# Two transformer blocks on one core: the mixing stage put into another order, attention ahead of the convolution

## What is computed

```python
x = x + 0.5 * swiglu(rms_norm(x, ffn1_norm[l]), ...)
h = rms_norm(x, mix_norm[l])
a, g, q, k, v = jnp.split(h @ w_in[l], splits, axis=-1)
# convolution branch: causal, per channel, 31 taps
u = a * jax.nn.sigmoid(g)
conv_out = jax.nn.silu(rms_norm(conv(u) + conv_b, conv_norm))
# attention branch: 4 heads, each with two score maps (d = 64), v of 128 columns
q, k = rms_norm(q, q_norm[l]), rms_norm(k, k_norm[l])
p = softmax(q @ k.T * scale + bias)          # causal, per head and map
o = (p[:, :, 0] - lam * p[:, :, 1]) @ v
diff_out = rms_norm(o, subln_g) * (1.0 - lam_init)
x = x + concat([conv_out, diff_out]) @ w_out[l]
x = x + 0.5 * swiglu(rms_norm(x, ffn2_norm[l]), ...)
```

## Time and profile before

| | us |
|---|---|
| median of 3 runs (1810.07 to 1811.17) | 1810.5 |
| the profiled execution, whole | 1811.22 |
| its span in the trace | 1809.4 |
| PE busy | 1758.0 (97%) |
| DVE busy | 1208.4 (67%) |
| ACT busy | 911.7 (50%) |
| POOL busy | 287.7 (16%) |
| granted TensorE clock, mean over the span | 0.992 |

### The profile page before, as it was taken

One profiled execution on the slowest core, in us unless ns is written; L12 is line 12 of the kernel. 1 busy time (PEld: TensorE's weight loads), 2 busy tenths in 40 slices (PEclk: granted clock), 3 DMA queues, 4 the chain that ended last, 5 costly groups with the idle time before them and its releaser, 6 DMA issues.

```text
span 1809.4 us, 25402 instructions
## 1 busy us (share of the span) xinstructions
PE 1758.0 (97%) x9839; PEld 1502.4 (83%) x9839; DVE 1208.4 (67%) x1594; ACT 911.7 (50%) x1221; POOL 287.7 (16%) x155
## 2 busy tenths in 40 slices
PE   8999999999999999999999998999999999989999
PEld 7757888899897788878888977888888889778887
DVE  5756766778676775576665794666666667946665
ACT  4544444545455444445445656544554456565443
POOL 2000300376241040000000741000000006410000
PEclk9999999999999999999999999999999999999999
DMA  9223655554502576535554432655465554316552
GB/s 302 102 70 124 220 191 186 152 181 156 198 1 83 156 238 194 188 129 195 194 193 163 164 116 70 209 185 188 161 209 185 186 185 164 117 47 209 192 194 102
DMA packets 203965, 293.95 MB, mean 162 GB/s; under 512 B 6426, under 2 KB 169728, under 8 KB 203888
## 3 DMA queue, kind: packets, MB, share of 16 engines
q1 hardware_dynamic: 200768, 285.62, 47.6%
q0 software_dynamic: 2688, 6.47, 1.4%
q10 hardware_dynamic: 432, 0.79, 0.1%
HBM read 291.81 MB, written 1.05 MB: 162 GB/s over the span
## 4 chain that ended last, share of the span: by engine, by line
PE 87%; DVE 8%; ACT 3%; issue 1%; DMA 0%; POOL 0%; SPq 0%; ACTq 0%; DVEq 0%
PE acc L1864 27%; PE pg L1864 15%; PE pg L1927 12%; PE pg L1931 12%; PE pg L1930 6%; PE pg L1928 6%; PE acc L2338 1%; DVE acc L1743 1%; PE pg L2134 1%; ACT w_hi L793 1%; DVE w_lo L1252 1%; PE pg L2322 1%; PE pg L2324 1%; DVE stats L1307 1%; PE pg L1975 1%
## 5 line engine op out<-in xcount | busy, mean ns | idle before, releaser
L1252 DVE TENSOR_TENSOR w_lo<-w_raw,w_hi 128x2048 fp32r<-128x2048 f32 x231 | 539.1, 2334 | 182.2 <-ACT w_hi L793 170.6
L793 ACT CAST w_hi<-w_raw 128x2048 fp32r<-128x2048 f32 x270 | 515.6, 1910 | 68.5 <-PE pg L1864 25.2
L1864 PE MATMUL acc<-w_hi,op 128*128 128x512 f32 x1536 | 496.6, 394 | 8.2 <-DVE op L1829 6.4
L1927 PE MATMUL pg<-op,w_hi 128*128 128x512 f32 x960 | 383.2, 399 | 7.7 <-DVE op L1278 3.8
L1931 PE MATMUL pg<-op,w_hi 128*128 128x512 f32 x960 | 380.8, 397 | 0.0
L1864 PEld LDWEIGHTS acc<-w_hi,op 128*128 128x128 f32 x1536 | 290.4, 189 | 70.0 <-issue 12.6
L1864 PE MATMUL acc<-w_lo,op 128*128 128x512 f32 x768 | 300.7, 392 | 0.0
L695 POOL TENSOR_TENSOR w_lo<-w_raw,w_hi 128x2048 fp32r<-128x2048 f32 x39 | 179.8, 4613 | 743.5 <-DVE w_lo L1252 615.4
L1930 PE MATMUL pg<-op,w_lo 128*128 128x256 f32 x960 | 267.9, 279 | 0.0
L1928 PE MATMUL pg<-op,w_lo 128*128 128x256 f32 x960 | 267.0, 278 | 0.0
L1864 PE MATMUL pg<-op,w_hi 128*128 128x256 f32 x1232 | 229.2, 286 | 2.8 <-DVE op L1278 1.2
(11 more groups left out here) (314 smaller groups left out, 1845.2 us busy)
## 6 DMA issues: line engine op xcount, KB each, us to landing
w_raw<-in_mlp_w SPq DMA_DIRECT2D x64, 1024.0 KB, 5.5
w_raw<-in_ffn_w_gate SPq DMA_DIRECT2D x44, 1024.0 KB, 5.1
w_raw<-in_ffn_w_up SPq DMA_DIRECT2D x44, 1024.0 KB, 5.1
w_raw<-in_ffn_w_down SPq DMA_DIRECT2D x44, 1024.0 KB, 4.8
w_raw<-in_ssm_w_in SPq DMA_DIRECT2D x24, 1024.0 KB, 5.3
w_raw<-in_w_in SPq DMA_DIRECT2D x20, 1024.0 KB, 5.0
w_raw<-in_attn_w_in SPq DMA_DIRECT2D x9, 1024.0 KB, 9.2
w_raw<-in_ssm_w_out SPq DMA_DIRECT2D x8, 1024.0 KB, 4.8
```

Of the source, the lines that this page charges most:

```text
L793: act.copy(w_hi[:, u % RING, :], w_raw[:, u % RING, :]).then_inc(hi_ready, 1)
L1252: dve.tensor_tensor(w_lo[:, s, :], w_raw[:, s, :], w_hi[:, s, :].bitcast(F32), ALU.subtract) \
L1864: ins = pe.matmul(psum, l, r, start=first and i == 0, stop=last and i == 2)
L1927: pe.matmul(bank, hi, joined, start=k == 0, stop=False)
```

## The change

The order of the units and of all four engines' programs in the mixing stage is new:

```diff
-MIX_COLS = [2 * U, 0, 3 * U, U] + [2 * CCH + i * U for i in (0, 2, 1, 3, 4, 5)]
-TAPS = [24, 22, 8, 8, 8, 8, 5, 5, 5]
-PE_TAPS = 6
-DIAGS = [0, 10, 20, CK]
+MIX_COLS = [2 * U, 0] + [2 * CCH + i * U for i in (0, 2, 1, 3)] + [3 * U, U] + [2 * CCH + i * U for i in (4, 5)]
+DIAGS = [0, 8, 16, 24, CK]
...
-                for n in range(OUT_UNITS):
-                    load(U_MIX_OUT[l] + n, rows(v_mix_out[l], n))
+                for n, g in enumerate((2, 3, 0, 1)):
+                    load(U_MIX_OUT[l] + n, rows(v_mix_out[l], g))
```

PE's program, the part that sets the order:

```diff
-                for s in range(2 * DH + 6):
-                    i = 8 * l + s
-                    if s < 2 * DH:
...
+                    if n == 6:
+                        score2(1)
+                    if n == 7:
+                        score2(3)
+                    feature_chunk(u, bank[:, T:2 * T], 1).then_inc(unit_done, 1)
+                    if n == 5:
+                        score2(0)
+                    if n == 6:
+                        score2(2)
+                        key_spread(2 * l + 1)
+                score2(4)
...
+                wide_tile(u, 0, acc[:, 0, :], 0)
+                score2(5)
+                pe.wait_ge(qk_ready, 2 * l + 2)
+                wide_tile(u, 0, acc[:, 1, :], 1).then_inc(unit_done, 1)
+                mix_turn(0)
+                score2(6)
+                take(u + 1)
+                wide_tile(u + 1, 1, acc[:, 0, :], 0).then_inc(first_tile, 1)
+                mix_turn(1)
+                score2(7)
+                wide_tile(u + 1, 1, acc[:, 1, :], 1).then_inc(unit_done, 1)
+                conv_taps(0, 4)
+                o2(l, 0)
+                mix_turn(2)
+                o2(l, 1)
```

DVE's and ACT's programs beside it, and block 1's two splits on ACT:

```diff
+                score_step(3)
+                mix_head(0)
                 gated_columns(1)
...
+                score_step(4)
+                mix_head(1)
+                convolve(3)
+                score_step(5)
+                convolve(4)
+                score_step(6)
+                convolve(2)
+                mix_head(2)
+                score_step(7)
...
+                gate_columns(1)
+                exp_step(0)
+                exp_step(1)
+                exp_step(2)
+                split(U_MIX[l] + 9)
+                exp_step(3)
+                split(U_MIX_OUT[l])
+                exp_step(4)
+                exp_step(5)
+                turned_mix(0)
+                split(U_MIX_OUT[l] + 1)
+                exp_step(6)
...
-                if s == AQ + 2:
-                    split(U_ATT_OUT + 2)
-                if s == AQ + 7:
-                    split(U_ATT_OUT + 3)
...
+                if s == 14:
+                    split(U_ATT_OUT + 2)
+                if s == 16:
+                    split(U_ATT_OUT + 3)
```

More of the change, by code:

```diff
@@ new lines, in _ @@
+                turned_mix(1)
+                exp_step(7)
+                link(act.activation(part[:, 0:1], lnb[:, 0:1], ACT.Sqrt))
+                act.wait_ge(unit_done, U_MIX[l] + 10)
+                act.copy(V2[:, 1, :], acc[:, 1, :]).then_inc(v_ready, 1)
+                turned_mix(2)
+                turned_mix(3)
+                o2_square(l, 0)
+                o2_square(l, 1)
+                o2_high(l, 0)
+                o2_high(l, 1)
+                split(U_MIX_OUT[l] + 2)
+                act.wait_ge(pe_conv, l + 1)
@@ new lines, in mix_turn, with conv_taps @@
+                def mix_turn(h):
+                    k = DH * l + h
+                    pe.wait_ge(mix_ready, k + 1)
+                    if h == 0:
+                        pe.wait_ge(gate_ready, 2 * l + 2)
+                    if k >= 1:
+                        pe.wait_ge(mixT_ready, k)
+                    for o in (0, P, 2 * P):
+                        ins = pe.transpose(pg[:, 2, o:o + P], pmix[:, k % 2, o:o + P], ident[:, :])
+                    ins.then_inc(mixT_done, 1)
+                def conv_taps(k0, k1):
+                    for k in range(k0, k1):
+                        if k == 0:
+                            pe.wait_ge(u_ready, 4 * l + 4)
+                        if k in DIAGS:
+                            pe.wait_ge(diag_ready, 4 * l + DIAGS.index(k) + 1)
+                        ins = pe.matmul(pg[:, 3, 0:T], diag_tap(k), uu[:, 3, k:k + T], start=k == 0, stop=k == CK - 1)
+                    if k1 == CK:
+                        ins.then_inc(pe_conv, 1)
@@ L2456, in _ @@
[L2456 to L2470 removed]
+                    elif n in (6, 7):
+                        pe.wait_ge(qk_sq, 4 * l + n - 5)
@@ new lines, in _ @@
+                    bank = pg[:, n % 4, :]
+                    if n < 3:
+                        project(u, bank, fresh=f"mix_{l}" if n == 0 else None)
+                        continue
+                    take(u)
+                    feature_chunk(u, bank[:, 0:T], 0)
+                    if n < 7:
+                        qk_sums(4 * l + n - 3)
+                    if n == 5:
+                        key_spread(2 * l)
+                    if n == 6:
+                        score2(1)
+                    if n == 7:
+                        score2(3)
@@ new lines, in _ @@
+                mix_turn(3)
+                o2(l, 2)
+                conv_taps(8, 12)
+                o2(l, 3)
+                conv_taps(12, 24)
+                o2_turn(0)
+                conv_taps(24, CK)
+                o2_turn(1)
+                u = U_MIX_OUT[l]
+                take(u)
+                pe.wait_ge(o2_ready, 2 * l + 1)
+                for i in (0, 1, 4, 5):
+                    output_part(u, 12, i, True, False)
+                pe.wait_ge(csq, 2 * l + 2)
+                for t in range(TT):
+                    for c in range(4):
+                        ins = pe.matmul(pg[:, 1, t:t + 1], osq[:, c, t * P:(t + 1) * P], ones_m,
+                                        start=c == 0, stop=c == 3)
@@ new lines, in _ @@
+                ins.then_inc(csum, 1)
+                take(u + 1)
+                pe.wait_ge(o2_ready, 2 * l + 2)
+                for i in (0, 1, 4, 5):
+                    output_part(u + 1, 14, i, False, False)
+                pe.wait_ge(crstd, l + 1)
+                for t in range(TT):
+                    ins = pe.matmul(pg[:, 1, T + t * P:T + (t + 1) * P], cdev[:, t:t + 1].broadcast_to([P, P]),
+                                    ident[:, :], start=True, stop=True)
+                ins.then_inc(cspread, 1)
```

564 lines of the change are left out of this document (286 added, 278 removed).

## The result

The changed kernel takes **1834.4 us** (median of 4 runs, 1834.14 to 1834.71) against 1810.8 for the kernel before, measured beside it: a ratio of 1.0131 (95% interval 1.0113 to 1.0148). The forecast was 1831, within 1814 to 1842.

The account below looks back on a forecast made before the run. PE, busy 97% of the span, bounds the kernel. 2 x (7.5 stage + 1.2 second feed-forward start + 2 slow clock) - 1 for block 1 = +20.4 on 1811.2 gives 1831.6; median 0.7 lower, 1831, range 1814 to 1842.

Parts of the forecast that it names:

- What decides: DVE beside POOL: DVE instructions reading data from SBUF alone wait for POOL's running subtraction, up to 4.6 us.
- Where it blocks: Scores among projections: multiplies L1832 and L1839 wait 4.4 and 4.6 us, L1832 of head 2 waits 3.4.
- its own sign of being wrong: If multiply L1832 is never above 0.5 us in the changed profile, the reason and the sign are wrong.
- PE's waits: Mixing stage to the out-projection's end: 3.6 + 2.7 + 1.1 + 3.3 + 7.3 + 3.1 = 21.1 us for 13.5.
- The stage's length: Mixing stage: out-projection ends at 133.5 for 126.0 in the layout, +7.5; about 135 to 139 us behind the warm-up.
- Slow clock: +2: Mixing stage, per layer: five waits of 2.7 to 7.3 us, about 5 us lost for 3; bounds 0 and 5.
- Block 1: PE's waits of 1.91 and 2.26 us behind casts that move later: -1 us, once; bounds -4.2 and +3.8.
- The turn: Start of the mixing stage: +0.2 us; PE waits 3.6 in place of 1.1 and works 1.8 less.
- PE's work: Mixing stage, per layer: 0 us, short matmuls of the sums taken at 0.11 each; lower end -4.
- The last taps: Convolution: chunk 2's last seven taps behind the attention's low halves, sums at 111.9 for 108.7, +3.1 us.
- The first (no block bites): Rival: DVE's multiplies start just before POOL or small ones pass; 1797 to 1808, say 1803; chance 0.15.
- The third (more bite): Rival: a lower clock moves steps into other subtractions; 5 us more a layer, 1842; chance 0.10.

Follow-up runs that it names:

- without POOL's length: Changed kernel with POOL subtracting only 8 of 2048 columns of each weight unit of the mixing stages, order and semaphores kept: 1807.4 us.
- the combined kernel: Changed kernel with three weight subtractions on DVE, the last seven taps early and ACT's root table load behind its copy of V: 1805.8 us.
- the last kernel: The combined kernel with the old turn, score steps earlier on DVE and chunk 2's taps dealt out around the attention's norm: 1795.7 us.

## Why the prediction was right, point by point

- **What decides.** Right, and shown: DVE's multiplies with source and destination in SBUF wait for POOL's subtraction, PE waits behind them (27 us between the changed kernel with and without POOL's length, 0.9 and within the noise in the kernel before). The prediction named the Trainium skill for it ("SBUF — State Buffer", section "Who interferes with whom"). By that rule the case agrees, with 0.16 us for a PSUM source and 3.78 for an SBUF source under one subtraction.
- **Where it blocks.** The size was right, the instruction was not: I laid 4.4 and 4.6 us on the mix of head 0 and 3.4 on that of head 2 (12.4); the trace has 3.9, 3.8 and 4.4 over the usual time on the last multiplies of steps 3, 4 and 6, 12.6 with the short one. POOL's subtraction started at 1047.38, 0.55 us ahead of step 3's multiply, where I had DVE 0.1 us ahead of POOL. When the source went to PSUM, the blocks fell where I had laid them. That the sums agree to 0.2 us is partly luck: by its own sign of being wrong (L1832 never above 0.5 us) the prediction would have been called wrong, as all eight L1832 took 0.23.
- **PE's waits.** I had 2.7 and 1.1 at the first transpose (measured none), 3.3 at the second (4.2), 7.3 at V (4.7), 3.1 at the sums (3.1): 17.5 for 12.0, with those of the turn 21.1 for 14.8. Part of this difference is the way of counting: the layout counts from when PE could issue, the trace from the end of the last matmul, as the prediction said of 13.5 and 8.2. Part is the clock: the layout has none, and with the clock kept up the gap at V is 3.44 + 4.11 = 7.6.
- **The stage's length.** The out-projection ended 141.5 us behind the warm-up, outside the 135 to 139 that I gave, +12.5 for +9.5. Of the half clock, 0.46 of the two short windows and 0.48 of PE's busy time in the two long ones is 8.6 us. 141.5 - 8.6 = 132.9 would meet the 133.5 laid out, but 2.7 of the 8.6 (0.48 of 5.53) lie ahead of V's wait and cost nothing. As an estimate, then, the clock cost about 5.9 us for 3.1 before, +2.8 for the "Slow clock: +2", and the stage without it is 135.6, 2 us longer than laid out. Which wait those 2 us belong to no run shows.
- **The slow clock: mis-sized in its sum.** Two waits with 3.1 us of lower clock behind them make 7.8 for five at the same price, not 5: the term was +4.7 by its own rule, and the whole about 1836. The windows have 8.6 us, and 20.5 and 23.9 us at half clock in the two layers for 6.8 and 10.2. But the rule itself does not hold: the first stretch of 6.83 us cost nothing, and that is why the +2 that I wrote down came out closer than the +4.7. This is luck.
- **Block 1: mis-sized.** -3.6 and not -1, which made good for part of the rest: 2 x 13.55 - 3.6 = +23.5 in the spans, for 2 x 10.7 - 1 = +20.4. With the -1 of the forecast the kernel would have been at about 1837.
- **The turn** cost 1.3 us a layer more than the old one, by the clock behind it, for 0.2. **PE's work** came out even: the 16 one-column matmuls of the convolution's sums took 2.12 us, a little above the upper bound of 0.11 each.
- **The last taps**, +3.1: right as a wait; with the clock behind it they were worth 5.2 a layer.
- **The rivals.** The first (no block bites) has an error in its sum: 7 to 12 us a layer below 1831 is 1807 to 1817, not 1797 to 1808. The kernel without POOL's length came to 1807.4, 13.5 a layer. The third (more bite) had its sign right in the clock, with a third of its size, but no further step moved into a subtraction: both layers have the same four. One reading was off by one as well: of the eight score steps of the kernel before, six and not seven lie behind 1066.96, and the first, at 1060.65, stands in a gap between two subtractions.

What stays open: the four parts of the loss were measured one at a time (POOL 27, taps 10.4, warm-up matmuls 9, and the turn 2.6 in the combined kernel) and overlap; they add up to more than the 24 us lost, since each also takes away some half clock of another. Not tried either: the repairs in the old order (the three subtractions on DVE, or the later load of the root's table), which might have gained there too.

## What to carry to other kernels

Before an instruction is moved on one engine, look at what the other engines do with SBUF at the new place: a multiply of two columns cost 4 us because a 1 MB subtraction of another engine had begun half a microsecond earlier. Where work on the slower engine cannot be moved out of the way, doing it on the waiting engine (2.3 us, once) beat being held up by it (up to 4.6 us, several times). A wait of PE can be worth more than its length, by the clock behind it (5.8 us between two layers with the same waits), but half clock ahead of another wait cost nothing. So ask at each stretch whether PE or another engine decides what comes next. And before a reordering is given credit, take out of it what would have helped the old order as well: here the two splits of block 1, which alone gave what the combined kernel gained.

## What the runs showed of the hardware beyond what was expected

- How much of an execution runs at half clock can differ between executions of one kernel, while the order of its instructions is the same: ten runs of the kernel with POOL cut short lie between 1801.7 and 1810.6, those above 1808.5 at a mean clock of 0.989 or 0.990, those below 1802.5 at 0.994 or 0.995. Long waits on PE alone do not make that spread: the changed kernel, whose longest wait is 4.7 us, has 0.6 us between its four runs, the last kernel, with none above 2 us in its first mixing stage, 2 us between its five. What decides it stays open.
- Matmuls of zeros in a wait, which only keep PE busy, gave back 9 us by the medians, 3 to 12.5 in single runs.
- A reciprocal that reads and writes SBUF alone ran at its usual 0.17 us under POOL's subtraction, where a multiply of two columns by a scalar waited to its end.
- The destination seems to count as well as the source. In the last kernel two multiplies by a scalar read SBUF and write PSUM while POOL's two subtractions run (to 1005.88). The two took 1.00 us together and were not held:

```profile
1004.80 1.00 DVE L1784 TENSOR_SCALAR acc<-arena,pcol 128x256 f32<-128x256 f32 x2
996.66 9.22 POOL L706 TENSOR_TENSOR w_lo<-w_raw,w_hi 128x2048 fp32r<-128x2048 f32 x2 [208.23 <-DVE w_lo L1300]
```

Those that waited wrote SBUF too, so the prediction's "reads its data from SBUF alone" was too wide. (These two also add a bias; no run changes the destination alone.)
